# Two blocks on one core: the last gate tiles moved between the first attention heads, the mixer's sums moved ahead of its states, the first weight block cut in four, and a last norm that GpSimd shares

## The reference, cut to what matters

```python
def hybrid_layer(h, p_i, positions, norm_g, w_in, b_f, qk_g, w_out, w_ple, ple_norm_g, w_ple_gate):
    z = rms_norm(h, norm_g) @ w_in                  # qa ka va ga fa qb kb vb gb
    ...
    oa = forgetting_attention(qa, ka, va, log_f) * jax.nn.silu(ga)     # 8 heads of 64
    ob = dilated_attention(qb, kb, vb) * jax.nn.silu(gb)               # 8 heads of 64
    h = h + jnp.concatenate([oa, ob], axis=-1) @ w_out
    gate = jax.nn.sigmoid(rms_norm(h, ple_norm_g) @ w_ple_gate)
    return h + (p_i @ w_ple) * gate

def second_block(x, mem, ...):
    for l in range(DEPTH):
        x = x + 0.5 * swiglu(rmsnorm(x, ffn1_norm[l]), ...)
        proj = rmsnorm(x, mix_norm[l]) @ w_in[l]
        o_a = hgrn2_mixer(...)     # S_t = diag(f_t) S_{t-1} + k_t v_t,  o_t = S_t^T q_t, 4 heads of 128
        o_b = multiscale_pool(...)
        x = x + jnp.concatenate([o_a, o_b], axis=-1) @ w_out[l]
        x = x + mem_cross_attention(...)
        x = x + 0.5 * swiglu(rmsnorm(x, ffn2_norm[l]), ...)
    return rmsnorm(x, final_norm)
```

## Time and profile before

| | us |
|---|---|
| timed runs, median | 3117.42 |
| timed runs, lowest and highest of 3 | 3112.37, 3121.12 |
| profiled execution, its own time | 3123.16 |
| its span, first to last instruction | 3121.3 |
| TensorE matmul busy in it | 3050.1 |

### The profile page before, as it was taken

The page is one execution under the profiler, slowest core; times in us unless marked ns, Lnnn a source line. Parts: engine busy times, 40 slices in busy tenths (PEclk is TensorE's granted clock), DMA queues, the critical chain, the costliest instruction groups (busy, mean ns, idle before and its releaser), DMA issues.

```text
span 3121.3 us, 33738 instructions
## 1 busy us (share of the span) xinstructions
PE 3050.1 (98%) x14426; PEld 2516.5 (81%) x14426; DVE 1641.3 (53%) x1870; ACT 1104.7 (35%) x1312; POOL 67.3 (2%) x70
## 2 busy tenths in 40 slices
PE   8999999999999999999999999999999999999998
PEld 6788877878888888888788888888888788788886
DVE  4455554555554557364455445645455463544545
ACT  5344444444422226333332222422235333432222
POOL 0000000000000000110000000000000200000000
PEclk9899999999999999999999999999999999999999
DMA  4110222102223223103222222222232014222221
GB/s 142 50 68 28 102 82 68 64 32 102 95 102 110 95 94 118 58 28 116 100 95 95 95 95 94 95 95 95 95 121 95 28 60 139 71 95 95 95 95 68
DMA packets 41493, 270.56 MB, mean 87 GB/s; under 512 B 5728, under 2 KB 5984, under 8 KB 9984
## 3 DMA queue, kind: packets, MB, share of 16 engines
q1 hardware_dynamic: 41344, 268.40, 24.7%
HBM read 266.22 MB, written 2.10 MB: 86 GB/s over the span
## 4 chain that ended last, share of the span: by engine, by line
PE 82%; DVE 10%; ACT 6%; issue 1%; DVEq 1%; DMA 0%; SPq 0%; ACTq 0%
PE PS L216 23%; PE PS L218 23%; PE PS L217 23%; DVE w_lo L201 4%; ACT w_hi L193 3%; PE PS L962 2%; PE PS L602 2%; DVE XT L1197 2%; PE PS L951 1%; PE PS L1708 1%; PE PS L1943 1%; PE PS L1969 1%; PE PS L1690 1%; DVE E L1619 1%; DVE total L280 0%
## 5 line engine op out<-in xcount | busy, mean ns | idle before, releaser
L193 ACT ACTIVATE w_hi<-w_raw 128x2048 fp32r<-128x2048 f32 x242 | 463.2, 1914 | 1202.8 <-PE PS L218 1198.8
L201 DVE TENSOR_TENSOR w_lo<-w_raw,w_hi 128x2048 fp32r<-128x2048 f32 x242 | 554.8, 2292 | 411.7 <-ACT w_hi L193 410.8
L216 PE MATMUL PS<-uh_b,w_hi 128*128 128x512 f32 x1312 | 512.2, 390 | 0.0
L218 PE MATMUL PS<-uh_b,w_lo 128*128 128x512 f32 x1312 | 511.1, 390 | 0.0
L217 PE MATMUL PS<-ul_b,w_hi 128*128 128x512 f32 x1312 | 510.9, 389 | 0.0
L216 PE MATMUL PS<-w_hi,uh_a 128*128 128x512 f32 x768 | 305.3, 398 | 14.4 <-DVE ul_a L271 10.9
L216 PE MATMUL PS<-uh_a,w_hi 128*128 128x512 f32 x800 | 313.7, 392 | 3.2 <-DVE ul_a L518 2.2
L218 PE MATMUL PS<-uh_a,w_lo 128*128 128x512 f32 x800 | 311.7, 390 | 0.0
L217 PE MATMUL PS<-ul_a,w_hi 128*128 128x512 f32 x800 | 311.6, 390 | 0.0
L217 PE MATMUL PS<-w_lo,uh_a 128*128 128x512 f32 x768 | 300.7, 392 | 0.0
L218 PE MATMUL PS<-w_hi,ul_a 128*128 128x512 f32 x768 | 300.3, 391 | 0.0
(11 more groups left out here) (294 smaller groups left out, 3786.8 us busy)
## 6 DMA issues: line engine op xcount, KB each, us to landing
w_raw<-in_weights SPq DMA_DIRECT2D x242, 1024.0 KB, 4.9
XT<-in_xT SPq DMA_DIRECT2D x8, 256.0 KB, 9.0
mem_raw<-in_mem SPq DMA_DIRECT2D x2, 1024.0 KB, 4.8
out<-XT SPq DMA_DIRECT2D x8, 256.0 KB, 2.0
bands<-in_bands SPq DMA_DIRECT2D x2, 768.0 KB, 6.4
mask_numbers<-in_masks SPq DMA_DIRECT2D x1, 1152.0 KB, 7.2
p_raw<-in_pT SPq DMA_DIRECT2D x2, 512.0 KB, 3.5
lb<-in_lb_logits SPq DMA_DIRECT2D x2, 512.0 KB, 5.8
```

Source lines behind the costliest of these rows:

```text
L193: act.activation(self.hi[g % 2][:], self.raw[g % 2][:], ACT.Copy).then_inc(self.hi_done.sem, 1)
L201: dve.tensor_tensor(self.lo[g % 2][:], self.raw[g % 2][:], self.hi[g % 2][:], ALU.subtract).then_inc(self.lo_done.sem, 1)
L216: pe.matmul(out, sh, mh, start=first, stop=False)
L218: return pe.matmul(out, sl, mh, start=False, stop=last)
```

## The change

1. **Opening.** Block 0 is loaded and split in four pieces of 512 columns, in turn with x tiles 0 to 3. Block 1 is loaded after x tile 7 instead of before x tile 2.
2. **Gates.** Of the gates' second block TensorE makes two token tiles at the old place, the third after the scores of head 1, the fourth after the transposes of head 0. ScalarE takes two tiles (Silu) after the exponentials of head 0, and two after those of head 1. VectorE waits for the gates only ahead of its first use of them.
3. **Mixer.** `sums(0)` goes ahead of decays and states, which follow it; the states use banks 5 to 7, the decays bank 4. The buffers `E` change places. VectorE does the pool's products ahead of `Kp`, and takes the states over after `weigh(0)`. The key transposes of heads 2 and 3 stand ahead of outputs(0) and outputs(1).
4. **Last norm.** Seven square buffers instead of two in the last feed-forward, whose last pair is added tile by tile. ScalarE applies the gain to tiles 6 and 7 and copies the row norm to SBUF; GpSimd multiplies tiles 6 and 7, VectorE tiles 0 to 5. The stores' order is 0 to 3, 6, 4, 5, 7.
5. Cross attention's semaphores are shared with those of other stages (names alone change).

```diff
@@ Weights
+    def load_piece(self, sp, j):
+        part = slice(j * 512, (j + 1) * 512)
+        sp.dma_start(self.raw[0][:, part], self.dram[0][:, part]).then_inc(self.piece_loaded[j].sem, 16)
...
+    def piece_split_hi(self, act, j):
...
+    def piece_split_lo(self, dve, j):
...
@@ Feed
     def square(self, act, c):
         act.wait_ge(*self.x.at(c + 1))
-        if c >= 3:
+        if c >= 3 and self.u:
             act.wait_ge(*self.summed.at(c - 2))
-        to = self.k.sq[c % 2] if c else self.k.total
+        to = self.square_of(c)
@@ Opening.sync
-        k.w.load_upto(sp, 1)
-        sp.dma_start(k.gains1[:], ins["gains1"]).then_inc(self.small.sem, 16)
-        sp.dma_start(k.XT[:, 0, :], ins["xT"][:, 0, :]).then_inc(self.x_arrived[0].sem, 16)
-        sp.dma_start(k.XT[:, 1, :], ins["xT"][:, 1, :]).then_inc(self.x_arrived[1].sem, 16)
+        sp.dma_start(k.gains1[:], ins["gains1"]).then_inc(self.gains_arrived.sem, 16)
+        for c in range(4):
+            k.w.load_piece(sp, c)
+            sp.dma_start(k.XT[:, c, :], ins["xT"][:, c, :]).then_inc(self.x_arrived[c].sem, 16)
+        for c in range(4, KD):
+            sp.dma_start(k.XT[:, c, :], ins["xT"][:, c, :]).then_inc(self.x_arrived[c].sem, 16)
         k.w.load_upto(sp, 2)
-        for c in range(2, KD):
-            sp.dma_start(k.XT[:, c, :], ins["xT"][:, c, :]).then_inc(self.x_arrived[c].sem, 16)
@@ Opening.scalar
         for c in range(KD):
+            if c < 4:
+                k.w.piece_split_hi(act, c)
+            if c == 0:
+                act.wait_ge(*self.gains_arrived.at(16))
             act.wait_ge(*self.x_arrived[c].at(16))
@@ HeadsProjection
+        for t in range(2):
+            self.take_gates(act, t)
+
+    def take_gates(self, act, t):
+        k = self.k
+        if t < NT - 1:
+            act.wait_ge(*self.g_done.at(t + 1))
+        else:
+            k.w.wait_used(act, self.g0 + 7)
+        act.activation(self.m.G[:, t, :], k.PS[:, 4 + t, :], ACT.Silu, scale=k.rt[:, t:t + 1]).then_inc(self.g_out.sem, 1)
...
         self.scores.products(pe, 0)
-        project(3, 1, 4)
+        w.ready(pe, g0 + 7)
+        for t in range(2):
+            self.last_gates(pe, t)
+
+    def last_gates(self, pe, t):
+
+        for c in range(4, KD):
+            i = split_products(pe, self.k.PS[:, 4 + t, :], [x[:, c, t * P:(t + 1) * P] for x in self.u],
+                               self.k.w.part(self.g0 + 7, (c - 4) * 512, 512), False, c == KD - 1)
+        i.then_inc((self.g_done if t < NT - 1 else self.k.w.used).sem, 1)
@@ HeadsAttention.scalar
             if h + 1 < NH:
                 self.scores.exps(act, h + 1)
+            if h == 0:
+                self.proj.take_gates(act, 2)
+                self.proj.take_gates(act, 3)
@@ HeadsAttention.vector
-        dve.wait_ge(*self.g_out.at(1))
...
+            if h == 1:
+                dve.wait_ge(*self.proj.g_out.at(NT))
@@ HeadsAttention.tensor
             if h == 0:
-                pe.wait_ge(*self.g_out.at(1))
+                self.proj.last_gates(pe, 2)
+                pe.wait_ge(*self.proj.g_out.at(2))
...
             turn(h)
+            if h == 0:
+                self.proj.last_gates(pe, 3)
+            if 1 <= h <= 2:
+                pe.wait_ge(*self.proj.g_out.at(2 + h))
             if h >= 1:
                 outputs(h - 1)
@@ FeedForward.vector, the last one
-            for pair in range(4):
+            for pair in range(3):
...
+            for c in (KD - 2, KD - 1):
+                if c == KD - 2:
+                    dve.wait_ge(*self.last_first.at(1))
+                else:
+                    w.wait_used(dve, self.down(last))
+                x = k.XT[:, c, :]
+                dve.scalar_tensor_tensor(x, k.PS[:, 4 + c % 4, :], 0.5, x, ALU.mult, ALU.add).then_inc(feed.x.sem, 1)
+                if c == KD - 2:
+                    feed.total(dve, 4)
+                    feed.total(dve, 5)
@@ PoolAndStates.vector: the three Kp products go behind the four pool products; take_states is called after weigh(0)
-        dve.tensor_copy(m.St[:, 0, :], k.PS[:, 4, :]).then_inc(self.state_read.sem, 1)
+        dve.tensor_copy(m.St[:, 0, :], k.PS[:, 5, :]).then_inc(self.state_read.sem, 1)
@@ Recurrence.tensor
+        turn_keys(0)
         pe.wait_ge(*self.states.mapped_read.at(4))
         sums(0)
+        pe.wait_ge(*self.kcopied.at(1))
+        self.states.decays(pe)
+        self.states.states(pe)
+        turn_keys(1)
         sums(1)
         for h in range(HH):
             scores(h)
+            if h + 2 < HH:
+                turn_keys(h + 2)
@@ Recurrence.tensor, scores
+                if h == 0 and unit < 2:
+                    pe.wait_ge(*self.states.state_read.at(unit + 1))
@@ Closing
     def sync(self, sp):
-        for c in range(KD):
+        for c in range(self.OWN):
             sp.wait_ge(*self.done.at(c + 1))
-            sp.dma_start(self.out[c * P:(c + 1) * P, :], self.k.XT[:, c, :]).then_inc(self.stored.sem, 16)
+            self.store(sp, c)
+            if c in (3, 5):
+                p = c // 4
+                sp.wait_ge(*self.pool_done.at(p + 1))
+                self.store(sp, self.OWN + p)
...
     def scalar(self, act):
+        k = self.k
+        for c in range(self.OWN, KD):
+            act.activation(k.XT[:, c, :], k.XT[:, c, :], ACT.Copy, scale=k.final_gain[:, c:c + 1]).then_inc(self.gained.sem, 1)
         self.rows.root(act)
+        self.rows.row(act)
...
-        dve.wait_ge(*self.rows.turned.at(1))
-        for c in range(KD):
-            dve.scalar_tensor_tensor(k.XT[:, c, :], k.XT[:, c, :], k.final_gain[:, c:c + 1], k.PS[:, self.rows.bank, :],
-                                     ALU.mult, ALU.mult).then_inc(self.done.sem, 1)
+        dve.wait_ge(*self.rows.row_ready.at(1))
+        for c in range(self.OWN):
+            dve.scalar_tensor_tensor(k.XT[:, c, :], k.XT[:, c, :], k.final_gain[:, c:c + 1], k.R[:], ALU.mult, ALU.mult)               .then_inc(self.done.sem, 1)
...
+    def gpsimd(self, pool):
+        k = self.k
+        pool.wait_ge(*self.gained.at(KD - self.OWN))
+        pool.wait_ge(*self.rows.row_ready.at(1))
+        for c in range(self.OWN, KD):
+            pool.tensor_tensor(k.XT[:, c, :], k.XT[:, c, :], k.R[:], ALU.mult).then_inc(self.pool_done.sem, 1)
```

More of the change, by code:

```diff
@@ L176, in __init__, with first_pieces, piece_ready @@
         self.next, self.hi_next, self.lo_next = 0, 0, 0
+    def first_pieces(self, sig):
+        self.piece_loaded = [sig(f"w_piece_loaded{j}", 16) for j in range(4)]
+        self.piece_hi, self.piece_lo = sig("w_piece_hi", 3), sig("w_piece_lo", 3)
+    def load_piece(self, sp, j):
+        part = slice(j * 512, (j + 1) * 512)
+        sp.dma_start(self.raw[0][:, part], self.dram[0][:, part]).then_inc(self.piece_loaded[j].sem, 16)
+        self.next = 1
+    def piece_split_hi(self, act, j):
+        part = slice(j * 512, (j + 1) * 512)
+        act.wait_ge(*self.piece_loaded[j].at(16))
+        act.activation(self.hi[0][:, part], self.raw[0][:, part], ACT.Copy)\
+           .then_inc((self.piece_hi if j < 3 else self.hi_done).sem, 1)
+        self.hi_next = 1
+    def piece_split_lo(self, dve, j):
+        part = slice(j * 512, (j + 1) * 512)
+        dve.wait_ge(*(self.piece_hi.at(j + 1) if j < 3 else self.hi_done.at(1)))
+        i = dve.tensor_tensor(self.lo[0][:, part], self.raw[0][:, part], self.hi[0][:, part], ALU.subtract)
+        i.then_inc((self.piece_lo if j < 3 else self.lo_done).sem, 1)
+        self.lo_next = 1
+    def piece_ready(self, pe, j):
+        if j < 3:
+            pe.wait_ge(*self.piece_lo.at(j + 1))
+        else:
+            self.ready(pe, 0)
     def load_upto(self, sp, end):
@@ L843, in tensor @@
         if self.rows:
-            project(0, 0, 0)
+            if g0 == 0:
+                for j in range(4):
+                    w.piece_ready(pe, j)
+                    self.u_ready(pe, j)
+                    for t in range(NT):
+                        i = split_products(pe, k.PS[:, t, :], [x[:, j, t * P:(t + 1) * P] for x in u], w.part(0, j * 512, 512),
+                                           j == 0, False)
+                i.then_inc(w.used.sem, 1)
+            else:
+                project(0, 0, 0)
             project(0, 1, 0, lambda pe, t: self.rows.sums(pe) if t == 1 else None)
@@ L1270, in down @@
                                            [x[:, j, :] for x in (m.h_hi[c % 2], m.h_lo[c % 2])], j == 0, j == 1)
+                    if not self.feed.u and c == NCHUNK - 1 and f == KD - 2:
+                        i.then_inc(self.last_first.sem, 1)
                 i.then_inc((self.pair_done if pair < 3 else w.used).sem, 1)
@@ L1540, in tensor, with take_decays, states @@
                 d = (c - 1) * HH + h
-                i = pe.matmul(k.PS[:, 7, d:d + 1], m.LF[:, c, h * P:(h + 1) * P], m.level[:, LEVELS * P + P - 1:LEVELS * P + P],
```

(27 more changed lines are left out.)

81 lines of the change are left out of this document (45 added, 36 removed).

## The result

The changed kernel takes 3082.43 us in the median of four runs (3080.89 to 3083.5). The kernel before, run beside it on the same chip, takes 3114.89 us (3109.17 to 3121.12). The ratio is 0.9895, with a 95% interval of 0.9874 to 0.9916. The profiled execution took 3082.03 us, its span is 3080.2 us.

A forecast was written before the change was run, and what follows sets the result against it. TensorE, busy 3050.1 of 3121.3 us, was taken as the bound, leaving its waits and half clock. Terms -1.2 - 24.1 - 17.0 + 1.4 = -40.9 took 3123.2 to 3082.3; the middle with 3076.6 gave 3079, range 3066 to 3093.

The forecast's parts named there:

- Opening, -1.2: Opening: TensorE starts 4.8 us sooner, column sums only 1.7 us sooner, 0.5 given back; -1.2 us, bounds -4 and +1.
- I take 14.2 for block 1: Opening: block 1, now last of the first 4 MB, lands at 14.2 us, bounds 13 and 15.5.
- I give back 0.5: Opening: 0.5 us lost to TensorE's 4.6 us idle ahead of the sums and eight small products perhaps at half clock.
- Gates, -24.1: Gates, four times: the stretches of 45.2, 33.5, 39.5 and 33.5 us shrink to 31.9 each, -24.1 us.
- two stalls (0.4 and 0.2): Gates: TensorE stalls about 0.4 us behind ScalarE's work, and 0.2 where outputs(0) wait for bank 6 to be read.
- the main choice: Gates: the clock stays up, since 0.6 us of gaps remain and a stretch with 2.2 us kept 1.00.
- Mixers, -17.0: Both mixers: weighing and output 0 come sooner, gaining 8.6 and 8.4 us; bounds per mixer 4 and 10.5.
- Last norm, +1.4: Last norm: 0.5 us sooner without contention, +2.0 from VectorE and GpSimd sharing SBUF; +1.4 us, bounds -0.5 and +2.5.
- I take the middle, 3079: Whole kernel: the profiled run was 5.7 us above the median, so 3079 us between 3082.3 and 3076.6.
- falls in the attentions: Attentions: the clock falls all the same in one or two, giving 3088 us (3085 to 3092); chance 0.23.
- late takeover: Mixers give half: the states' takeover behind the weighing holds up scores(0) and the clock falls; +9, 3088 us; chance 0.09.
- The slower rival: Attentions: the clock falls in every one at the first table load and stays down; 3152 us with 14 heads; chance 0.02.

The follow-up runs named there:

- experiment 3: The changed kernel with block 0 loaded in one transfer again, as before the change: 3078.92 us, ratio 0.988.
- Experiments 8: The changed kernel with all four gate tiles ahead of head 1's products, Silu still tile by tile, VectorE's wait still at head 1: 3099.59 us, ratio 0.9967.
- kernels 9: The changed kernel with the third gate tile back ahead of head 1's scores, the fourth still behind head 0's transposes: 3080.09 us, ratio 0.9887.
- kernel 10: The changed kernel with three gate tiles ahead of head 1's scores and the fourth between them and head 0's transposes: 3114.99 us, ratio 1.0006.
- experiment 6: The changed kernel with VectorE's six last-norm multiplications reading the row from PSUM, GpSimd still from SBUF: 3080.67 us, ratio 0.9889.
- kernel 12: The changed kernel with later column sums, last-norm multiplications all on VectorE from PSUM, and block 0 in one transfer: 3073.73 us, ratio 0.9873.
- 11: The changed kernel with column sums behind block 1's sixth chunk and all eight last-norm multiplications on VectorE from PSUM: 3073.02 us, ratio 0.987.
- kernels 1: The changed kernel with the whole gates edit reversed, four tiles in a row and one wait for all: 3102.15 us, ratio 0.9963.

## Why the prediction was right, step by step

The forecast of 3079 lay 3.4 us below the measured 3082.4, and the sum of its terms, 3082.3 for the profiled execution, met 3082.03. That is partly luck: four terms missed by 1.7 to 2.2 us each, two in either direction.

- **Opening, -1.2: wrong sign, +1.0** against the profile of before and 2.6 us against the old opening in a profile without a fall of the clock (experiment 3). The step that failed is "I take 14.2 for block 1, since the queue is filled a little sooner": it landed at 15.76, outside the bounds of 13 and 15.5; the last of the same 4 MB had landed at 15.28 before, and filling the queue sooner moved nothing forward. The other is "I give back 0.5" for the idle time: the wait came as predicted, 4.4 us for 4.6, though by luck, since TensorE started 1.4 us later than "near 6" and the sums 1.6 later than 23.9; but half clock followed for some 7 us, not only for the eight small products. The upper bound of +1 just held.
- **Gates, -24.1: -26.0 in the profiles.** 31.4 us for the predicted 31.9; the count of ScalarE's work (10.8 us) was right, TensorE's was 10.9 instead of 10.4, so of the two stalls (0.4 and 0.2) only one came, 0.3 us ahead of outputs(0), and for the gates, not for bank 6. Experiments 8 to 10 show that it hangs on one tile, the one behind head 0's transposes, which the step did not single out. The clock stayed at 1.00, the main choice. The size is right only for the execution that was profiled: in the medians the gates bring 19.7.
- **Mixers, -17.0: -19.1.** The order of events came as predicted, 8.0 us from `ul_a` to the weighing for 8.15, 26.4 us to sums(2) for 26.8. The term was undersized: the two mixers themselves gained 9.4 and 11.1 us, the second more than its bound of 10.5, and 1.7 were lost again in the cross attention.
- **Last norm, +1.4: +3.1.** The contention was priced right, 2.0 us over six tiles for 2.0, and experiment 6 shows that it is contention. The copy to R cost the 0.6 us that were counted, and the square buffers gained 0.3. What the step left out is the stores' rate: it gave the stores 0.4 us more, and they took 2.1 more (4.6 us behind VectorE's last product, 2.5 before), which is the whole miss of 1.7. The 1.34 us that it credited for two tiles less on VectorE are not there to be had when the queues carry one tile in 0.66 us.
- **"I take the middle, 3079": wrong.** Its own argument was that the changed kernel hardly depends on the run once the half clock is gone; then the counted 3082.3 stands for every run and nothing is to be taken off. So it was: the four runs lie within 2.6 us, and what scatters is the kernel before (16 us over the 17 runs beside kernels 9 and 10).
- **Rivals.** None of the falls in the attentions and no late takeover came about in the profiled execution. The slower rival's mechanism is real: kernel 10, with one pause of 2.1 us in each attention, is as slow as the kernel before. What is to be seen was seen, but for the first matmul, at 7.4 us instead of 6, and the sums, at 25.5 instead of 23.9.

## What to carry to other kernels

Where TensorE's clock falls behind pauses, look for the one piece of independent work that fits into the longest pause: here a tile of 2.7 us behind head 0's transposes carried the gates' 20 us, and a second tile moved with it carried nothing that shows. An early start is worth only what the next dependency lets through, and a wait that it lengthens can cost more than it brought; move the waiting instruction behind work that doesn't need it first. Before a second engine shares the last step, compare the first engine's time for a tile with the rate at which the stores leave, and see whether both read their operands from SBUF.

## What the runs showed of the hardware

A pause of the same length, at the same place of the program, was followed by half clock in one kernel's profile and not in another's. The wait for `PTm` of 2.0 us was in the changed kernel and not in kernel 12, 1.0 us for `w_lo` was in 11 and not in 12. Within one kernel it varies too: kernels 1, 8 and 10 spread over 16 to 28 us without a change of code, their mean granted clock going with the time (kernel 10: 0.988 or 0.989 at 3107 to 3111 us, 0.982 or 0.983 at 3124 to 3127). What decides it was not found. Kernels 11 and 12 differ in their openings alone and still differ by two falls of 1.7 us each far behind them, be it by the shift or by chance, so an edit's own worth is read at the end of its own stage and not in the total. In both places where a core moved megabytes at once, the first loads and the last stores, it moved 388 to 407 GB/s in windows of 2 or 4 us in which the queues were full. A VectorE product of 128x512 with two operands in SBUF took 1.75 us beside a GpSimd product that reads SBUF, and 0.74 us (0.66 from start to start) alone or with one operand in PSUM; GpSimd's took 1.7 to 1.8 beside it and 1.3 otherwise.
